# Where the last norm's token rows are fetched, and which rows of the last expert are finished first, in a diffusion step with a mixture of experts

## The chip, the cores and the metric

The kernel runs on one core of a Trainium2 chip. The metric is the device time of one launch in microseconds (us). The kernel before took 1339.0 us (the median of three runs, 1337.55 to 1339.12).

A few words that the text uses: TensorE is PE in the profile (PEld is its weight load), VectorE is DVE, ScalarE is ACT, GpSimd is POOL, and SyncE is SP, which computes nothing here and only issues transfers. PSUM is where TensorE leaves its sums.

## The reference

One inference step: a trunk layer over 512 sample tokens and 128 prompt tokens of width 1024, then a routed layer of 16 experts, then a last norm. What bears on the change is the end:

```python
def ec_moe(x, router_w, w1, w3, w2):
    probs = softmax(xf @ router_w)
    gates, idx = lax.top_k(probs.T, cap)        # cap: 64 sample tokens, 16 prompt tokens per expert
    xe = xf[idx]
    h = silu(xe @ w1) * (xe @ w3)               # 1024 -> 2048, for each of 16 experts
    ye = (h @ w2) * gates                       # 2048 -> 1024
    return zeros.at[idx].add(ye)

x = x + gate2 * ec_moe(h2, ...)
y = x * rsqrt(mean(x * x) + EPS) * final_norm_w   # rmsnorm of every token row
```

The outputs are the normed rows of the prompt and of the sample tokens, and two final states of the trunk's scan.

## The kernel before

**The trunk** takes about the first quarter of the time and is not touched. It leaves the token rows (5 tiles of 128 rows by 1024; tile 4 holds the prompt rows) in DRAM, in `acc_dram`.

**The experts.** Each expert has 12 weight pieces of 2 MB: eight for w1 and w3 (`m` 0 to 7), four for w2 (`m` 8 to 11). SP issues them in order into a ring of six slots (L596) and waits, before each, until TensorE has read the piece six before it. Expert 0 stands by itself, experts 1 to 14 are a loop, and the last one (15, `LAST`) stands by itself. Every expert but the last adds its rows to `acc_dram` with a scatter from GpSimd (L749).

**The last expert.** Its rows are not scattered into `acc_dram`. GpSimd gathers the rows concerned (`last_rows`, the sample rows, L753; `last_rows_p`, the 16 prompt rows, L756) as soon as expert 14's scatter has landed, VectorE adds the last expert's products to them, and they get their own norm. TensorE takes the products in this order: the sample part of w2's first piece (`down_sample(0)`, L1289), the prompt part of all four pieces (`down_prompt(i)`, L1300), and then the sample part of the other three. So the prompt products (`Y_B` in PSUM) are complete first and the sample products (`Y_A`) last.

**The tiles.** Meanwhile all 640 rows as experts 0 to 14 left them are normed too: SP fetches the five tiles of `acc_dram` into `x` (L641, `acc_loaded`), ScalarE squares and sums each (L1638, `y_squared`), VectorE makes mean and reciprocal (L1664, L1665, `y_recip`), ScalarE takes the root (L1640, `y_rs`), VectorE scales the five tiles (`scale_tiles`, L2165, `y_ready`), and SP stores them (L650, `y_saved`). The rows that the last expert has also changed are stale in these stores and are overwritten: GpSimd scatters the prompt rows (L764) and the sample rows (L768) over them. L764 waits for `y_saved` of all five tiles and for `last_p_scaled`; L768 stands behind L764 in GpSimd's program and waits for `last_scaled`.

**VectorE at the end.** `finish_prompt_rows` adds the rows (L2171), waits for ScalarE's square (L1643), makes mean and reciprocal, waits for the root (L1645) and scales (L2175). `finish_sample_rows` reads `Y_A` (L2181), adds (L2185), waits for ScalarE's square (L1647) and a small TensorE product that sums two half rows (L1369), makes mean and reciprocal, waits for the root (L1649) and scales (L2190).

**What sets the order** is the order in which the code is written. Every engine works through its own program in order, and whatever waits for a semaphore holds up all that stands behind it on its engine. No planner takes part.

Of the kernel before, what the change touches and what calls it, by code (L numbers as in the profile page):

```python
# [18 lines left out]
ACT = mybir.ActivationFunctionType  # L19
# [5 lines left out]
P = 128  # L25
# [3 lines left out]
TILES = (SAMPLE + PROMPT) // P  # L29
# [11 lines left out]
CAP_S, CAP_P = 2 * SAMPLE // EXPERTS, 2 * PROMPT // EXPERTS  # L41
# [3 lines left out]
LAST = EXPERTS - 1  # L45
# [116 lines left out]
OUT_ORDER = [ST] + list(range(ST))  # L162
# [33 lines left out]
def trunk_kernel(nc, x_prompt, x_sample, s0_f, s0_b, c, c_ctx, ada_w, ada_b, norm1_w, w_in, wa2_f, ba_f,  # L196
                 wa2_b, ba_b, gla_norm_w, sgu_norm_w, sgu_ws, sgu_bs, w_out, norm2_w, router_w, w1, w3, w2,
                 final_norm_w, table, pos_row, pos_col, y_prompt, y_sample, new_f, new_b):
    with ExitStack() as ctx:
# [27 lines left out]
        x = sb("x", TILES * D)[:].rearrange("p (t d) -> p t d", t=TILES)  # L227
# [338 lines left out]
        def _(sp):  # L566
# [68 lines left out]
                    wait_expert_chunk_read(sp, m - RING, expert)  # L635
                    load_expert_chunk(m, expert)
            for m in range(EXPERT_LOADS):
                if m == 9:
                    sp.wait_ge(acc_saved, 16 * (TILES + LAST))
                    for t in OUT_ORDER:  # L640
                        sp.dma_start(x[:, t, :], acc_dram[t * P:(t + 1) * P, :]).then_inc(acc_loaded[t], 16)  # L641
                wait_expert_chunk_read(sp, m - RING, LAST)
                load_expert_chunk(m, LAST)


            for i, t in enumerate(OUT_ORDER):
                sp.wait_ge(y_ready, i + 1)
# [725 lines left out]
        def _(act):  # L1373
# [259 lines left out]
                expert_work(expert)  # L1633
            expert_work(LAST)

            for i, t in enumerate(OUT_ORDER):
                act.wait_ge(acc_loaded[t], 16)
                nc.scalar.activation(y_out[:, t, :], x[:, t, :], ACT.Square, accum_out=stats[:, 130 + i:131 + i]).then_inc(y_squared, 1)  # L1638
            act.wait_ge(y_recip, 1)
            nc.scalar.activation(stats[:, 140:140 + TILES], stats[:, 135:135 + TILES], ACT.Sqrt).then_inc(y_rs, 1)  # L1640

            act.wait_ge(last_p_added, 1)
            nc.scalar.activation(last_sq_p, last_rows_p, ACT.Square, accum_out=stats[0:CAP_P, 145:146]).then_inc(last_p_squared, 1)  # L1643
            act.wait_ge(last_p_recip, 1)
            nc.scalar.activation(stats[0:CAP_P, 148:149], stats[0:CAP_P, 147:148], ACT.Sqrt).then_inc(last_p_rs, 1)  # L1645
            act.wait_ge(last_added, 1)
            nc.scalar.activation(last_sq, last_rows, ACT.Square, accum_out=stats[:, 125:126]).then_inc(last_squared, 1)  # L1647
            act.wait_ge(last_recip, 1)
# [4 lines left out]
        def _(dve):  # L1653
# [8 lines left out]
            def mean_recip(out, sums, width, then, own=link):  # L1662

                own(nc.vector.tensor_scalar(out, sums, 1.0 / width, EPS, ALU.mult, ALU.add))  # L1664
                nc.vector.reciprocal(out, out).then_inc(then, 1)  # L1665
# [492 lines left out]
            def scale_tiles():  # L2158

                dve.wait_ge(y_squared, TILES)  # L2160
                mean_recip(stats[:, 135:135 + TILES], stats[:, 130:130 + TILES], D, y_recip, link_final)
                dve.wait_ge(final_loaded, 16)
                dve.wait_ge(y_rs, 1)
                for i, t in enumerate(OUT_ORDER):
                    nc.vector.scalar_tensor_tensor(y_out[:, t, :], x[:, t, :], stats[:, 140 + i:141 + i], final_w, ALU.mult, ALU.mult)\  # L2165
                        .then_inc(y_ready, 1)

            def finish_prompt_rows():

                dve.wait_ge(last_p_loaded, 16)  # L2170
                nc.vector.tensor_tensor(last_rows_p, last_rows_p, last_y_p[0:CAP_P], ALU.add).then_inc(last_p_added, 1)  # L2171
                dve.wait_ge(last_p_squared, 1)
                mean_recip(stats[0:CAP_P, 147:148], stats[0:CAP_P, 145:146], D, last_p_recip, link_final)
                dve.wait_ge(last_p_rs, 1)
                nc.vector.scalar_tensor_tensor(last_rows_p, last_rows_p, stats[0:CAP_P, 148:149], final_w[0:CAP_P], ALU.mult, ALU.mult)\  # L2175
                    .then_inc(last_p_scaled, 1)
# [15 lines left out]
            def expert_work(expert, last=False):  # L2192
# [9 lines left out]
                for part in range(PARTS):  # L2202
# [5 lines left out]
                    wait_role_stored(dve, f"R3_{part}", expert)  # L2208
                    nc.vector.transpose(h[:, :, part * PART:(part + 1) * PART], h_rows[:, part, :].rearrange("p (c a) -> p c a", a=PART))\  # L2209
                        .then_inc(h_turned[part], 1)  # L2210
                if last:
                    scale_tiles()
                else:
                    dve.wait_ge(gathered, 16 + 48 + expert * 48)
                    for part in range(PARTS):
                        ins = nc.vector.transpose(xe[:, :, part * PART:(part + 1) * PART], xq[:, part, :].rearrange("p (i k) -> p k i", k=KT))  # L2216
                    ins.then_inc(xq_turned, 1)
                    dve.wait_ge(xq_turned, expert + 1)
                    kinds = ((slice(0, CAP_S), 0), (slice(CAP_S, PADDED), 1))
                    for slots, w in kinds:  # L2220
                        shape = [P, KT, slots.stop - slots.start]
                        ins = nc.vector.tensor_tensor(xe[:, :, slots], xe[:, :, slots], amp2[:, :, w:w + 1].to_broadcast(shape), ALU.mult)
                    link_expert(ins)
                    for slots, w in kinds:
                        shape = [P, KT, slots.stop - slots.start]
                        ins = nc.vector.tensor_tensor(xe[:, :, slots], xe[:, :, slots], mod[:, SHIFT2:SHIFT2 + KT, w:w + 1].to_broadcast(shape),
                                                      ALU.add)
                    ins.then_inc(xe_ready, 1)
# [13 lines left out]
                if last:  # L2242
                    link_final(ins)
                    finish_prompt_rows()
                    finish_sample_rows()
                    return
                wait_role_filled(dve, "Y_A", expert)
# [38 lines left out]
```

## Time and profile before

| | |
|---|---|
| median of three runs | 1339.0 us |
| the profiled execution: its own time, its span | 1340.9 us, 1339.1 us |
| TensorE busy | 1323.7 us (99% of the span) |
| VectorE busy | 462.6 us (35%) |
| ScalarE busy | 170.5 us (13%) |
| GpSimd busy | 109.4 us (8%) |
| moved by the DMA engines | 470.88 MB, 352 GB/s over the span |
| the last weight piece, from issue to landing | 1297.22 to 1319.1 us |
| last matmul of the last expert | ends at 1331.35 us |

The span runs from the first to the last instruction of the profiled execution; the own time of that execution also holds what lies around it. A time such as 1319.1 us is counted from the span's start. The mean busy shares are averages over the trunk, sixteen experts and the end; the change lies in the last 60 us alone.

### The profile page before, as it was taken

How to read it: one execution, taken by the hardware profiler on the slowest of the kernel's cores; microseconds unless marked ns; L12 is line 12 of the kernel's file. 1: busy time of each engine (PE TensorE's matmuls, PEld its weight loads, DVE VectorE, ACT ScalarE, POOL GpSimd, SP SyncE). 2: the span in 40 equal slices, each digit the busy share in tenths (PEclk: the TensorE clock that was granted, in tenths of full speed). 3: DMA queues.
4: the chain of work that ended last, by engine and by line, in shares of the span. 5: the costliest groups of instructions: out<-in, count | busy, mean ns of one | idle time of the engine just before them, and what ended most of it. 6: DMA issues, size and time to landing. Idle time of an engine off the chain costs nothing.

```text
span 1339.1 us, 24267 instructions
## 1 busy us (share of the span) xinstructions
PE 1323.7 (99%) x10761; PEld 470.6 (35%) x10761; DVE 462.6 (35%) x850; ACT 170.5 (13%) x277; POOL 109.4 (8%) x119
## 2 busy tenths in 40 slices
PE   9999999999999999999999999999999999999996
PEld 3544555554333333333333333333333333333331
DVE  3189886977130403122121304031221212130405
ACT  3443624123100000000000000000000000000002
POOL 0300000110100101010000001010100000000000
PEclk9999999999999999999999999999999999999999
DMA  9733731247799999999999999999999999999995
GB/s 316 252 126 134 251 111 36 83 157 288 278 424 421 424 419 415 431 417 428 418 427 419 426 419 426 420 421 426 414 431 415 429 418 426 420 427 418 430 406 221
DMA packets 64349, 470.88 MB, mean 352 GB/s; under 512 B 5685, under 2 KB 17794, under 8 KB 39738
## 3 DMA queue, kind: packets, MB, share of 16 engines
q1 hardware_dynamic: 57184, 451.56, 81.4%
q0 software_dynamic: 6320, 18.45, 4.6%
q8 instruction: 26, 0.43, 0.1%
q10 hardware_dynamic: 810, 0.37, 0.1%
q14 instruction: 9, 0.07, 0.0%
HBM read 456.99 MB, written 13.37 MB: 351 GB/s over the span
## 4 chain that ended last, share of the span: by engine, by line
PE 95%; DMA 2%; DVE 1%; issue 1%; ACT 0%; POOL 0%; POOLq 0%; DVEq 0%
PE psum L1273 49%; PE psum L1289 15%; PE psum L1300 8%; PE psum L843 8%; PE psum L1117 4%; PE psum L885 2%; PE psum L1059 2%; DMA ring<-in_exp_w_dram 2%; PE psum L850 1%; PE psum L930 1%; PE psum L1069 1%; PE psum L863 1%; PE psum L786 0%; PE psum L1023 0%; PE psum L1028 0%
## 5 line engine op out<-in xcount | busy, mean ns | idle before, releaser
L1273 PE MATMUL psum<-ring,both 128*32 128x512 f32 x6144 | 664.8, 593 | 0.6 <-issue 0.6
L1273 PEld LDWEIGHTS psum<-ring,both 128*32 128x32 f32 x6144 | 199.4, 110 | 457.5 <-issue 457.3
L2205 DVE TENSOR_TENSOR both<-both,psum 128x512 f32<-128x512 f32 x48 | 50.4, 1051 | 555.7 <-PE psum L1273 555.7
L1289 PE MATMUL psum<-ring,both 128*32 128x512 f32 x2048 | 231.1, 592 | 0.0
L1626 ACT ACTIVATE both<-psum 128x512 f32<-128x512 f32 x48 | 28.7, 597 | 934.0 <-PE psum L1273 934.0
L1300 PE MATMUL psum<-ring,both 128*32 128x512 f32 x1024 | 118.6, 592 | 2.9 <-DMA ring<-in_exp_w_dram 2.9
L1289 PEld LDWEIGHTS psum<-ring,both 128*32 128x32 f32 x2048 | 66.6, 110 | 153.2 <-issue 153.2
L843 PE MATMUL psum<-ring,feat 128*128 128x512 f32 x240 | 104.3, 593 | 0.0
L701 POOL DMA_INDIRECT both<-xn_dram,both x45 | 49.5, 1101 | 579.2 <-DVE both L2216 569.8
L2235 DVE SCALAR_TENSOR_TENSOR both<-psum,both 64x512 f32<-64x512 f32 x32 | 24.0, 749 | 177.7 <-PE psum L1300 177.5
L1117 PE MATMUL psum<-ring,both 128*128 128x512 f32 x160 | 71.2, 596 | 0.0
L843 PEld LDWEIGHTS psum<-ring,feat 128*128 128x128 f32 x240 | 45.1, 190 | 55.2 <-issue 55.1
L1300 PEld LDWEIGHTS psum<-ring,both 128*32 128x32 f32 x1024 | 33.1, 110 | 80.1 <-issue 75.4
L1712 DVE SCALAR_TENSOR_TENSOR both<-ring,silu_c,both 128x512 f32<-128x512 f32 x88 | 58.8, 744 | 0.0
L749 POOL DMA_INDIRECT acc_dram<-both x15 | 22.0, 1467 | 267.2 <-DVE both L2250 267.2
L1117 PEld LDWEIGHTS psum<-ring,both 128*128 128x128 f32 x160 | 29.5, 190 | 32.9 <-issue 32.9
L2209 DVE STREAM_TRANSPOSE both<-both 128x512 f32<-128x512 f32 x48 | 34.2, 712 | 1.7
L885 PE MATMUL psum<-feat,ring 128*128 128x512 f32 x64 | 29.1, 597 | 0.0
L1059 PE MATMUL psum<-feat,ring 128*128 128x512 f32 x64 | 28.0, 596 | 0.0
L2216 DVE STREAM_TRANSPOSE both<-both 128x256 f32<-128x256 f32 x45 | 25.2, 605 | 0.0
L2250 DVE SCALAR_TENSOR_TENSOR both<-psum,both 64x512 f32<-64x512 f32 x30 | 22.5, 750 | 6.7 <-PE psum L1289 6.5
L2241 DVE TENSOR_TENSOR both<-both 32x512 f32<-32x512 f32 x32 | 21.9, 684 | 0.8
(312 smaller groups left out, 632.3 us busy)
## 6 DMA issues: line engine op xcount, KB each, us to landing
ring<-in_exp_w_dram SPq DMA_DIRECT2D x192, 2048.0 KB, 17.6
ring<-in_ada_w_dram SPq DMA_DIRECT2D x8, 2048.0 KB, 7.9
ring<-in_w_in_dram SPq DMA_DIRECT2D x4, 2048.0 KB, 14.5
ring<-in_ada_w_dram SPq DMA_DIRECT2D x6, 1024.0 KB, 11.3
ring<-in_w_out_dram SPq DMA_DIRECT2D x2, 2048.0 KB, 12.2
acc_dram<-x POOLq DMA_DIRECT2D x5, 512.0 KB, 3.1
xn_dram<-feat POOLq DMA_DIRECT2D x5, 512.0 KB, 5.2
x<-acc_dram SPq DMA_DIRECT2D x5, 512.0 KB, 18.0
```

The lines of the kernel that those rows point to most:

```text
L701: pool.indirect_dma_start(out=xq[:, part, :], out_offset=None, in_=xn2_dram.rearrange("t (a n) -> (t a) n", a=4), in_offset=bass.IndirectO ...
L843: mm = nc.tensor.matmul(bank(n), hT[:, kt, t * P:(t + 1) * P], w[:, kt, :], start=(kt == 0), stop=(kt == KT - 1))
L885: return nc.tensor.matmul(bank(JOB["qkS", m]), w[:, kt, m * P:(m + 1) * P], hT[:, kt, 0:SAMPLE], start=(kt == 0), stop=(kt == KT - 1))
L1059: mm = nc.tensor.matmul(bank(n), w[:, kt, gr * P:(gr + 1) * P], hT[:, kt, 0:SAMPLE], start=(kt == 0), stop=(kt == KT - 1))
L1117: mm = nc.tensor.matmul(bank(n), mix, w[:, kt, :], start=(kt == 0), stop=(kt == KT - 1))
L1273: mm = nc.tensor.matmul(role_bank(role)[f4 * PART:(f4 + 1) * PART, :], xe[:, kt, part * PART:(part + 1) * PART], w[:, kt % 2, f4 * 512:(f4 ...
L1289: mm = nc.tensor.matmul(role_bank("Y_A")[at:at + PART, :], h[:, c, part * PART:(part + 1) * PART], w[:, f, half * 512:(half + 1) * 512], s ...
L1300: mm = nc.tensor.matmul(role_bank("Y_B")[at:at + PART, :], h[:, c, 2 * PART:PADDED], w[:, f + odd, half * 512:(half + 1) * 512], start=(c ...
L1626: role_stored(nc.scalar.activation(silu_h[:, r % 2, :], role_bank(role), ACT.Silu), role)
L1712: ins = nc.vector.scalar_tensor_tensor(sums[:, w, :], rows[:, kt, :], scale, sums[:, w, :], ALU.mult, ALU.add)
L2205: role_stored(nc.vector.tensor_tensor(h_rows[:, part, :].rearrange("p (c a) -> p a c", a=PART), silu_h[:, part % 2, :].rearrange("p (a c) ...
L2209: nc.vector.transpose(h[:, :, part * PART:(part + 1) * PART], h_rows[:, part, :].rearrange("p (c a) -> p c a", a=PART))\
```

## The change

Three things are moved. SP fetches the five tiles behind the last expert's last weight piece, no longer ahead of its tenth. ScalarE's square and root for the prompt rows stand ahead of the squares of the tiles. On VectorE, `scale_tiles` is called behind `finish_prompt_rows` and ahead of `finish_sample_rows`, and the wait for the norm's weight row (`final_loaded`) goes along to the first scaling. No instruction is added or removed.

```diff
@@ SP, the last expert's weight pieces
             for m in range(EXPERT_LOADS):
-                if m == 9:
-                    sp.wait_ge(acc_saved, 16 * (TILES + LAST))
-                    for t in OUT_ORDER:
-                        sp.dma_start(x[:, t, :], acc_dram[t * P:(t + 1) * P, :]).then_inc(acc_loaded[t], 16)
                 wait_expert_chunk_read(sp, m - RING, LAST)
                 load_expert_chunk(m, LAST)
-
+            sp.wait_ge(acc_saved, 16 * (TILES + LAST))
+            for t in OUT_ORDER:
+                sp.dma_start(x[:, t, :], acc_dram[t * P:(t + 1) * P, :]).then_inc(acc_loaded[t], 16)
@@ ScalarE, behind the last expert's work
+            act.wait_ge(last_p_added, 1)
+            nc.scalar.activation(last_sq_p, last_rows_p, ACT.Square, accum_out=stats[0:CAP_P, 145:146]).then_inc(last_p_squared, 1)
+            act.wait_ge(last_p_recip, 1)
+            nc.scalar.activation(stats[0:CAP_P, 148:149], stats[0:CAP_P, 147:148], ACT.Sqrt).then_inc(last_p_rs, 1)
             for i, t in enumerate(OUT_ORDER):
                 act.wait_ge(acc_loaded[t], 16)
                 nc.scalar.activation(y_out[:, t, :], x[:, t, :], ACT.Square, ...).then_inc(y_squared, 1)
             act.wait_ge(y_recip, 1)
             nc.scalar.activation(stats[:, 140:140 + TILES], stats[:, 135:135 + TILES], ACT.Sqrt).then_inc(y_rs, 1)
-            act.wait_ge(last_p_added, 1)
-            nc.scalar.activation(last_sq_p, last_rows_p, ACT.Square, ...).then_inc(last_p_squared, 1)
-            act.wait_ge(last_p_recip, 1)
-            nc.scalar.activation(stats[0:CAP_P, 148:149], stats[0:CAP_P, 147:148], ACT.Sqrt).then_inc(last_p_rs, 1)
@@ VectorE, expert_work(LAST, last=True)
-                if last:
-                    scale_tiles()
-                else:
+                if not last:
...
                 if last:
                     link_final(ins)
                     finish_prompt_rows()
+                    scale_tiles()
                     finish_sample_rows()
                     return
```

ScalarE's program behind the last `silu` of the last expert, before. `acc_loaded4` is the prompt tile, `last_p_added` says that VectorE has added the prompt rows:

```order
L1638 ACTIVATE feat,stats<-x 128x1024 [waits acc_loaded4]
L1638 ACTIVATE feat,stats<-x 128x1024 [waits acc_loaded0]
L1638 ACTIVATE feat,stats<-x 128x1024 [waits acc_loaded1]
L1638 ACTIVATE feat,stats<-x 128x1024 [waits acc_loaded2]
L1638 ACTIVATE feat,stats<-x 128x1024 [waits acc_loaded3]
L1640 ACT_TABLE_LOAD
L1640 ACTIVATE stats<-stats 128x5 [waits y_recip]
L1643 ACTIVATE both,stats<-both 16x1024 [waits last_p_added]
L1645 ACTIVATE stats<-stats 16x1 [waits last_p_recip]
L1647 ACTIVATE both,stats<-both 128x512 [waits last_added]
```

The same place on ScalarE in the changed kernel (its lines are numbered anew: 1635 is the prompt rows' square, 1640 the tiles'):

```order
L1635 ACTIVATE both,stats<-both 16x1024 [waits last_p_added]
L1637 ACT_TABLE_LOAD
L1637 ACTIVATE stats<-stats 16x1 [waits last_p_recip]
L1640 ACTIVATE feat,stats<-x 128x1024 [waits acc_loaded4]
L1640 ACTIVATE feat,stats<-x 128x1024 [waits acc_loaded0]
L1640 ACTIVATE feat,stats<-x 128x1024 [waits acc_loaded1]
L1640 ACTIVATE feat,stats<-x 128x1024 [waits acc_loaded2]
L1640 ACTIVATE feat,stats<-x 128x1024 [waits acc_loaded3]
L1642 ACTIVATE stats<-stats 128x5 [waits y_recip]
L1645 ACTIVATE both,stats<-both 128x512 [waits last_added]
```

The prompt rows' two instructions have moved to the front, the load of the root's table has gone with the first root, and the five squares of the tiles now stand behind a wait for `last_p_added`.

VectorE's program behind the last transpose of the last expert, before. `psum_filled7` says that the prompt products `Y_B` are complete, `psum_filled6` the sample products `Y_A`:

```order
L1664 TENSOR_SCALAR stats<-stats 128x5 [waits y_squared]
L1665 RECIPROCAL stats<-stats 128x5 [waits vec_final_step]
L2165 SCALAR_TENSOR_TENSOR feat<-x,stats,both 128x1024 [waits y_rs,final_loaded]
L2165 SCALAR_TENSOR_TENSOR feat<-x,stats,both 128x1024 x4
L2235 SCALAR_TENSOR_TENSOR both<-psum,both 64x512 [waits psum_filled7,acc_saved]
L2235 SCALAR_TENSOR_TENSOR both<-psum,both 64x512
L2241 TENSOR_TENSOR both<-both 32x512 [waits psum_stored7]
L2241 TENSOR_TENSOR both<-both 32x512
L2171 TENSOR_TENSOR both<-both 16x1024 [waits last_p_loaded,vec_final_step]
L1664 TENSOR_SCALAR stats<-stats 16x1 [waits last_p_squared]
L1665 RECIPROCAL stats<-stats 16x1 [waits vec_final_step]
L2175 SCALAR_TENSOR_TENSOR both<-both,stats 16x1024 [waits last_p_rs]
```

The same place in the changed kernel, from the prompt rows' addition to the reading of `Y_A` (2168 was 2171, 2162 was 2165, 2179 was 2181):

```order
L2168 TENSOR_TENSOR both<-both 16x1024 [waits last_p_loaded,vec_final_step]
L1662 TENSOR_SCALAR stats<-stats 16x1 [waits last_p_squared]
L1663 RECIPROCAL stats<-stats 16x1 [waits vec_final_step]
L2173 SCALAR_TENSOR_TENSOR both<-both,stats 16x1024 [waits last_p_rs,final_loaded]
L1662 TENSOR_SCALAR stats<-stats 128x5 [waits y_squared]
L1663 RECIPROCAL stats<-stats 128x5 [waits vec_final_step]
L2162 SCALAR_TENSOR_TENSOR feat<-x,stats,both 128x1024 [waits y_rs]
L2162 SCALAR_TENSOR_TENSOR feat<-x,stats,both 128x1024 x4
L2179 SCALAR_TENSOR_TENSOR both<-psum,both 128x512 [waits psum_filled6]
```

The tiles' mean, reciprocal and five scalings have moved from ahead of the prompt products to between the prompt rows and the sample rows.

## Rows read from the trace of the kernel before

**Rows 1.** The page: busy time, share of the span and instructions of each engine.

```profile
PE 1323.7 (99%) x10761; PEld 470.6 (35%) x10761; DVE 462.6 (35%) x850; ACT 170.5 (13%) x277; POOL 109.4 (8%) x119
```

**Rows 2.** The chain that ended last, in order of time: start us, us, what.

```profile
1297.22 21.87 DMA ring<-in_exp_w_dram
```

**Rows 3.** Timeline of SP's issues: start us, us, engine, line, operation, tiles, count.

```profile
1286.92 10.63 SPq L596 DMA_DIRECT2D ring<-in_exp_w_dram  x3
1314.53 5.58 SPq L650 DMA_DIRECT2D out_dram<-feat  x5
```

**Rows 4.** Line 641, the last tile's fetch alone: duration ns, start; time to landing.

```profile
L641 SPq DMA_DIRECT2D x<-acc_dram x1: 432/432/432, 1284.8 to 1284.8; - x1
...
DMA to landing us min/median/max: 19.6/19.6/19.6
```

**Rows 5.** Line 596, the piece issued at 1286.92 alone: its time to landing.

```profile
DMA to landing us min/median/max: 22.4/22.4/22.4
```

**Rows 6.** Timeline of PEld around the last two pieces' prompt products; brackets: idle before.

```profile
1313.28 0.13 PEld L1300 LDWEIGHTS psum<-ring,both 128*32 128x32 f32 x4 [0.30 <-issue]
...
1319.13 0.16 PEld L1300 LDWEIGHTS psum<-ring,both 128*32 128x32 f32 x8 [3.85 <-DMA ring<-in_exp_w_dram]
...
1320.44 0.13 PEld L1289 LDWEIGHTS psum<-ring,both 128*32 128x32 f32 x4 [0.30 <-issue]
```

**Rows 7.** Timeline of ACT and DVE in the tiles' norm.

```profile
1306.30 1.05 ACT L1638 ACTIVATE feat<-x 128x1024 f32<-128x1024 f32 x1
...
1311.61 1.28 ACT L1640 ACT_TABLE_LOAD   x1
...
1312.91 0.21 ACT L1640 ACTIVATE stats<-stats 128x5 f32<-128x5 f32 x1
1313.22 6.07 DVE L2165 SCALAR_TENSOR_TENSOR feat<-x,stats,both 128x1024 f32<-128x1024 f32 x5 [1.20 <-ACT stats L1640]
```

**Rows 8.** Timeline of ACT and DVE over the prompt rows.

```profile
1321.19 1.51 DVE L2235 SCALAR_TENSOR_TENSOR both<-psum,both 64x512 f32<-64x512 f32 x2 [1.91 <-PE psum L1300]
...
1324.15 1.21 DVE L2171 TENSOR_TENSOR both<-both 16x1024 f32<-16x1024 f32 x1
...
1325.39 1.06 ACT L1643 ACTIVATE both<-both 16x1024 f32<-16x1024 f32 x1 [12.28 <-DVE both L2171]
...
1326.36 0.18 ACT L1643 ACTIVATION_READ_ACCUMULATOR both<-both 16x1 f32 x1
...
1326.93 0.20 ACT L1645 ACTIVATE stats<-stats 16x1 f32<-16x1 f32 x1 [0.39 <-DVE stats L1665]
...
1327.17 1.27 DVE L2175 SCALAR_TENSOR_TENSOR both<-both,stats 16x1024 f32<-16x1024 f32 x1 [0.27 <-ACT stats L1645]
```

**Rows 9.** Timeline over the sample rows and the last scatter.

```profile
1331.42 0.75 DVE L2181 SCALAR_TENSOR_TENSOR both<-psum,both 128x512 f32<-128x512 f32 x1 [2.98 <-PE psum L1289]
...
1333.80 0.35 PE L1369 MATMUL psum<-stats,fold 128*128 128x1 f32 x2 [2.44 <-ACT both L1647]
...
1334.82 0.75 DVE L2190 SCALAR_TENSOR_TENSOR both<-both,stats 128x512 f32<-128x512 f32 x1 [0.27 <-ACT stats L1649]
1335.85 1.02 POOL L768 DMA_INDIRECT out_dram<-both  x1 [5.70 <-DVE both L2190]
```

**Rows 10.** Line 650, all five stores of the tiles: their time to landing.

```profile
DMA to landing us min/median/max: 3.8/4.2/5.9
```

**Rows 11.** Line 695, five stores of 512 KB in the trunk: their time to landing.

```profile
DMA to landing us min/median/max: 3.0/3.1/11.3
```

**Rows 12.** Timeline of POOL: both gathers of the last rows, and the prompt rows' scatter.

```profile
1278.44 1.01 POOL L753 DMA_INDIRECT both<-acc_dram,both  x1 [8.89 <-DMA acc_dram<-both]
1279.75 0.90 POOL L756 DMA_INDIRECT both<-acc_dram,both  x1 [0.30 <-issue]
1329.28 0.86 POOL L764 DMA_INDIRECT out_dram<-both  x1 [48.63 <-DVE both L2175]
```

**Rows 13.** One stretch: busy us and count of each engine, granted clock, DMA share, GB/s.

```profile
1334.00:1336.00 2.00, 0.15 (x2) 0.07 (x1) 1.08 (x3) 0.20 (x1) 0.15 (x1) 0.58 0.00 0
```

More of the change, by code:

```diff
@@ L1640, in _ @@
             nc.scalar.activation(stats[:, 140:140 + TILES], stats[:, 135:135 + TILES], ACT.Sqrt).then_inc(y_rs, 1)
-            act.wait_ge(last_p_added, 1)
-            nc.scalar.activation(last_sq_p, last_rows_p, ACT.Square, accum_out=stats[0:CAP_P, 145:146]).then_inc(last_p_squared, 1)
-            act.wait_ge(last_p_recip, 1)
-            nc.scalar.activation(stats[0:CAP_P, 148:149], stats[0:CAP_P, 147:148], ACT.Sqrt).then_inc(last_p_rs, 1)
             act.wait_ge(last_added, 1)
@@ L2161, in scale_tiles @@
                 mean_recip(stats[:, 135:135 + TILES], stats[:, 130:130 + TILES], D, y_recip, link_final)
-                dve.wait_ge(final_loaded, 16)
                 dve.wait_ge(y_rs, 1)
@@ L2173, in finish_prompt_rows @@
                 mean_recip(stats[0:CAP_P, 147:148], stats[0:CAP_P, 145:146], D, last_p_recip, link_final)
+                dve.wait_ge(final_loaded, 16)
                 dve.wait_ge(last_p_rs, 1)
```

## The prediction

> **What bounds the kernel now.** I read the page first: TensorE is busy for 99% of the span [rows 1], so only its waits and what runs behind its last product can be won or lost. Then the chain of waits, and in it the last 60 us, since the change touches nothing earlier. The reader should see one wait that isn't TensorE's own work: the last weight piece, issued at 1297.22, lands 21.87 us later, at 1319.09 [rows 2]. The timeline of the weight loads shows what it costs. A group of four loads comes every 0.43 us (0.13 and 0.30 idle). From the group at 1313.28 to the first one of the sample products at 1320.44 are 7.16 us [rows 6]. Eight groups lie between (the prompt products of the last two pieces, 16 each, four to a group), so unhindered it is nine pitches, 3.87 us. The stall is 7.16 - 3.87 = 3.29 us.
>
> Behind the stall comes a serial end: the prompt products are read at 1321.19 [rows 8], the sample products at 1331.42, the last scatter starts at 1335.85 [rows 9], and the span ends 3.25 us later, at 1339.1. The tiles' own norm, from 1306.30 to 1319.29 [rows 7], is hidden now: ScalarE and VectorE have nothing else to do while TensorE works and waits. That cover is what the change gives up.
>
> **Part 1, SP: the tiles behind the last piece.** Line 641's five issues go past three weight pieces. The last tile, issued at 1284.8, lands 19.6 us later, at 1304.4 [rows 4]. The piece behind it, issued at 1286.92 [rows 3], lands after 22.4 us, at 1309.3 [rows 5]. So 2048 KB took 4.9 us behind a tile, and the five tiles of 512 KB are worth 2560/2048 x 4.9 = 6.1 us. Each of the last three pieces lands that much earlier, the last one at 1313.0. TensorE wants it at 1313.28 + 5 x 0.43 = 1315.4, so there are 2.4 us to spare and the stall goes whole: -3.29 us for both sets of products. It can't be more, since TensorE wants the piece no earlier. SP now waits for `acc_saved` behind the last piece; that was met before 1278.44, when the gathers started [rows 12], and costs nothing. Behind it are only the stores. The tiles land from about 1314.2 to 1319.1 (1313.0 + 6.1).
>
> At the queue a rule bears on this. The trace shows pieces and tiles landing in the order of issue. The Trainium skill, "DMA: Bandwidth & Descriptors", section "Queues, rings and completion order", says the same of the start of descriptors on one engine, but also that completions of one issuing engine are not first in, first out. By its first half the last piece is clear of the tiles; by its second it need not be, which is the first rival below.
>
> **Part 2, ScalarE: prompt rows first.** Two costs. First, all five squares now stand behind `last_p_added` and the prompt root. With the stall gone, VectorE reads the prompt products at 1321.19 - 3.29 = 1317.90. By [rows 8] the prompt square starts 4.20 us later (1325.39 - 1321.19) and ends at +5.35 (1326.36 + 0.18), so at 1323.25. Second, the table load, 1.28 us [rows 7], now lies here: it doesn't wait for the semaphore of the root (in the tiles' norm it starts at 1311.61, when the squares end). So it runs 1323.27 to 1324.55, beside VectorE's two small instructions, and the root ends at 1324.77. Without the load it would have ended at 1317.90 + 5.94 = 1323.84, so this costs 0.93 us. The tiles have long landed (5.7 us to spare), and the five squares take 1311.61 - 1306.30 = 5.31 us: to 1330.08.
>
> A rule speaks for more. Between load and root the row leaves 0.02 us (1311.61 + 1.28 to 1312.91) [rows 7]. The Trainium skill, "ScalarE: Activation LUTs", section "What ACT_TABLE_LOAD costs", puts a drain of about 1380 ns beside the load of about 1283 ns. By the row the sum stays; by the rule the tiles' norm would be later by about 1.4 us. I take the row.
>
> **Part 3, VectorE: tiles between prompt and sample rows.** From the end of a square over mean, reciprocal and root to the scaling are 1327.17 - 1326.54 = 0.63 us without a load [rows 8], so the five scalings start at 1330.71 and with their 6.07 us [rows 7] end at 1336.78. Queued behind them is the reading of `Y_A` (complete at about 1328.1) and the whole sample part, for which ScalarE, TensorE's last small product and the last scatter wait. It starts at 1336.8, not at 1331.42 - 3.29 = 1328.13. `L2190` ends 4.15 us after that start (1334.82 + 0.75 - 1331.42), and the scatter could start 4.43 us after it (1335.85 - 1331.42) [rows 9]: 1341.2. That alone makes an end at 1344.5. Moving `final_loaded` costs nothing: that row was fetched in the first third of the kernel.
>
> **Part 4, the stores and the order of the scatters.** The five stores are not added, but lose their cover. The last is issued at 1336.8. Its landing took 3.8 to 5.9 us beside the weights [rows 10]; the same 512 KB took 3.0 to 3.1 us in the trunk where nothing was in the way, up to 11.3 otherwise [rows 11]. Nothing else is under way now and a store is shorter (about 1.2 us by part 1) than a scaling, so I take 3.1: 1339.9; the ends are 3.0 and 5.9. GpSimd's scatter L764 waits for it and started 0.84 us after its releaser before (L2175 ended at 1328.44), L768 0.28 us after its own; I take 0.6. L768 stands behind L764, and two such issues follow at 1279.75 - 1278.44 = 1.31 us [rows 12]. So L768 starts at 1339.9 + 0.6 + 1.31 = 1341.8, 0.6 later than VectorE would let it, and the span ends 3.25 us later: 1345.1. That the prompt rows are finished ahead (1326.1 for 1328.44) brings nothing, because L764 waits for the stores.
>
> TensorE idles 11 us ahead of its small product. Before, after 2.44 us idle, it took 0.35 us [rows 9], and the mean granted clock of the stretch around the end was 0.58 [rows 13]. At the lower level (1.2 of 2.4 GHz) it and its weight load of 0.30 us cost at most 0.65 us more, and at least nothing. I take nothing, since up to 0.6 us hides behind the stores.
>
> **The sum.** Span 1339.1 to 1345.1: -3.29 for the stall, +8.67 for the sample part behind the tiles (1336.8 - 1328.13), +0.6 for the stores. The profiled execution's own time is 1340.9 and would be 1346.9. It lies 1.9 above the median of 1339.0; the same +6.0 gives **1345.0 us**. The ends: stores at 3.0 and 0.28 of lag give 1344.5 for the median, 5.9 and 0.84 give 1348.0.
>
> **Rival 1: the stall stays.** The tiles share the engines with the last piece, which is issued just ahead of them, and it lands at 1319.1 as before. For it speaks that the stores issued from 1314.53 [rows 3] landed from 3.8 us on [rows 10], the first at 1318.3, ahead of the last piece. Against it, that a piece behind the tiles took 4.9 us, its full share of the stream. Everything is then 3.29 later: 1348.3.
>
> **Rival 2: a longer load of the table.** In its new place it is followed by a pause as long as itself, 1.28 us. Only the 0.02 us after it speaks against. 1346.3.
>
> **Rival 3, the other side: the last products carry the end, and the stall's 3.29 comes out whole,** 1335.7. It needs the passes over the tiles to be much shorter once the DMA engines are quiet. The point from which it isn't slower: the sample part starts by 1331.42, so squares and scalings must lose 5.4 of their 11.4 us. Against it: the prompt rows' square (1.06) and scaling (1.27) ran when the weights had ended [rows 8] and are as long as those of a tile (1.05, and 6.07 for five) [rows 7].
>
> **How the numbers follow.** Forecast 0.83, rival 1 0.09, rival 2 0.04, rival 3 and its half-way cases 0.04. A measurement here tells 0.2%, 2.7 us, from no change. The forecast and the first two rivals are all slower by more; of the last 0.04 I give 0.01 to faster and 0.03 to no change. The range runs from 1342.9, below the lowest sum (1344.5) by the scatter of the runs (1.6 us), to 1348.5, which takes in rival 1 and the late stores.
>
> **What would show it.** Right: no wait of TensorE for a weight piece in the last expert; the prompt products read near 1317.9; the table load between the prompt square and its root; squares of the tiles from about 1324.8, their scalings from 1330.7 to 1336.8; L2179 (the former L2181) released by nothing but its place; L764 near 1340.5, released by the stores, and L768 right behind it. Wrong: a wait for the last piece that stays (rival 1), a gap behind the table load (rival 2), tile passes under 1 us each (rival 3), or a last scatter that starts before 1339.

## The result and the profile after

The changed kernel takes 1345.07 us (median of six runs, 1344.79 to 1348.03) against 1339.09 us (six runs, 1337.55 to 1341.57). The ratio is 1.0047, with a 95% interval from 1.0037 to 1.0057: slower by 5.0 to 7.6 us. The forecast was 1345.0 us.

The profiled execution has a span of 1343.1 us. That is only 4.0 us more than 1339.1, because this execution was 1.5 us ahead already when the last expert's second half began. So the traces are compared from one point that no variant touches: the start of the last expert's first sample product (`down_sample(0)`). In the trace of before it is here (timeline of PE: start us, us, what):

```profile
1307.27 3.62 PE L1289 MATMUL psum<-ring,both 128*32 128x512 f32 x32
```

From there to the end of the span are 31.83 us. In the changed kernel the same stretch begins and goes on like this (timeline of PE and SP; L1287 is the former L1289, L1298 the former L1300, L642 the former L641):

```profile
1296.07 2.33 SPq L642 DMA_DIRECT2D x<-acc_dram  x5
...
1305.76 3.62 PE L1287 MATMUL psum<-ring,both 128*32 128x512 f32 x32
...
1309.19 7.05 PE L1298 MATMUL psum<-ring,both 128*32 128x512 f32 x64
...
1316.06 10.48 PE L1287 MATMUL psum<-ring,both 128*32 128x512 f32 x96
```

From 1305.76 to 1343.1 are 37.34 us: +5.51 (spans are recorded to 0.1 us; up to the start of the last scatter the difference is 5.52, from 28.58 to 34.10). All 64 matmul rows of the prompt products are now one piece without a gap, where before 48 of them were followed by the wait that [rows 6] show. The last piece's time from issue to landing, 21.87 us in [rows 2], is now

```profile
L596 SPq DMA_DIRECT2D ring<-in_exp_w_dram x1: 328/328/328, 1295.7 to 1295.7; - x1
...
DMA to landing us min/median/max: 15.7/15.7/15.7
```

and that is 6.2 us less. What the stall gave back, the end took, and more. This is the chain that ended last, from the prompt square on, in order of time (start us, us, what):

```profile
1320.58 1.15 ACT both L1635 x2
1321.72 0.02 issue
1321.74 1.28 ACT L1637
1323.02 0.01 issue
1323.04 0.20 ACT stats L1637
1323.24 5.20 ACT feat L1640 x10
...
1330.34 4.88 DVE feat L2162 x4
1335.21 0.02 issue
1335.23 3.04 DMA out_dram<-feat
1338.26 0.27 issue
1338.53 0.86 POOL out_dram L762
```

The reader should see that TensorE's sample products are nowhere in it, though the last of them ended only at 1326.54 (1316.06 + 10.48): prompt square, table load, root, the five squares of the tiles (x10 with their accumulator reads), the five scalings. Before, the squares [rows 7] were not in this chain. From 1335.23 on the view goes over the last store and the prompt rows' scatter. What released the last scatter was VectorE's last scaling (L2188, in the last row below), and that stands behind the sample part and TensorE's small product; the run with TensorE busy shows below that this second way was the longer one, by little. The rows that answer to [rows 8], [rows 9] and [rows 12], from the timeline (L2231 reads the prompt products, L2162 scales the tiles, L2179 starts the sample part, L1367 is the small product):

```profile
1316.38 1.51 DVE L2231 SCALAR_TENSOR_TENSOR both<-psum,both 64x512 f32<-64x512 f32 x2 [8.51 <-PE psum L1298]
...
1329.13 6.07 DVE L2162 SCALAR_TENSOR_TENSOR feat<-x,stats,both 128x1024 f32<-128x1024 f32 x5 [0.28 <-ACT stats L1642]
...
1335.23 0.75 DVE L2179 SCALAR_TENSOR_TENSOR both<-psum,both 128x512 f32<-128x512 f32 x1
...
1337.61 0.56 PE L1367 MATMUL psum<-stats,fold 128*128 128x1 f32 x2 [11.07 <-ACT both L1645]
...
1338.83 0.75 DVE L2188 SCALAR_TENSOR_TENSOR both<-both,stats 128x512 f32<-128x512 f32 x1 [0.27 <-ACT stats L1647]
1339.86 1.02 POOL L766 DMA_INDIRECT out_dram<-both  x1 [0.47 <-DVE both L2188]
```

The sample part (L2179) has no idle time before it: it waited only for its place behind the scalings.

### The profile page after: what moved, and what is told of

It reads as the page before. It is cut to its first block, busy times and chain, and to the rows that moved or that the text cites. A ratio compares the mean times of both kernels' runs of the same rounds, so it can differ in the third digit from the quotient of the medians.

```text
span 1343.1 us, 24267 instructions
## 1 busy us (share of the span) xinstructions
PE 1319.6 (98%) x10761; PEld 470.0 (35%) x10761; DVE 462.3 (34%) x850; ACT 170.4 (13%) x277; POOL 109.3 (8%) x119
## 4 chain that ended last, share of the span: by engine, by line
PE 95%; DVE 2%; DMA 1%; SPq 1%; ACT 1%; issue 1%; POOLq 0%; POOL 0%; DVEq 0%
PE psum L1271 49%; PE psum L1287 16%; PE psum L1298 8%; PE psum L841 8%; PE psum L1115 4%; PE psum L883 2%; PE psum L1057 2%; DMA ring<-in_ada_w_dram 1%; PE psum L1067 1%; PE psum L928 1%; SPq L578 1%; PE psum L784 0%; PE psum L1021 0%; ACT feat L1640 0%; PE psum L1026 0%
## 5 line engine op out<-in xcount | busy, mean ns | idle before, releaser
L1287 PE MATMUL psum<-ring,both 128*32 128x512 f32 x2048 | 231.1, 592 | 0.0
L1287 PEld LDWEIGHTS psum<-ring,both 128*32 128x32 f32 x2048 | 66.6, 110 | 153.2 <-issue 153.2
L1298 PE MATMUL psum<-ring,both 128*32 128x512 f32 x1024 | 118.3, 592 | 0.0
L2231 DVE SCALAR_TENSOR_TENSOR both<-psum,both 64x512 f32<-64x512 f32 x32 | 24.0, 750 | 184.3 <-PE psum L1298 184.0
L1298 PEld LDWEIGHTS psum<-ring,both 128*32 128x32 f32 x1024 | 33.3, 110 | 76.6 <-issue 76.6
```

The costliest lines, as they stand in the source:

```text
L1287: mm = nc.tensor.matmul(role_bank("Y_A")[at:at + PART, :], h[:, c, part * PART:(part + 1) * PART], w[:, f, half * 512:(half + 1) * 512], s ...
L1298: mm = nc.tensor.matmul(role_bank("Y_B")[at:at + PART, :], h[:, c, 2 * PART:PADDED], w[:, f + odd, half * 512:(half + 1) * 512], start=(c ...
```

## The experiments

Two theories stood. The one of the forecast: the tiles' fetch costs a stall of 3.3 us where it was, its new place gives that back, and VectorE's and ScalarE's passes over the tiles, put between the prompt rows and the sample rows, cost 8.7 us. The rival: the late fetch itself, with its late stores, is what costs.

The variants were timed in five rounds beside the kernel before on the same chip (1339.67 us in the first set of four, 1338.72 us in the second, of the last three timed ones), all but the two with a busy TensorE, which ran once each. The ratio is against the kernel before of the same set. "Stretch" is the time in the trace from the start of the last expert's first sample product to the end of the span, which is known to 0.1 us.

| kernel | time us | ratio and 95% interval | stretch us | against before |
|---|---|---|---|---|
| before | 1339.09 | | 31.83 | |
| changed | 1345.07 | 1.0047, 1.0037 to 1.0057 | 37.34 | +5.51 |
| only the fetch moved | 1343.24 | 1.0028, 1.0018 to 1.0037 | 35.67 | +3.84 |
| only the orders moved | 1349.20 | 1.0073, 1.0060 to 1.0085 | 40.13 | +8.30 |
| changed, squares first | 1341.19 | 1.0009, 1.0000 to 1.0019 | 33.44 | +1.61 |
| before, no fetch (output incomplete) | 1334.90 | 0.9967, 0.9955 to 0.9979 | 28.54 | -3.29 |
| two tiles ahead | 1335.43 | 0.9976, 0.9965 to 0.9987 | 28.56 | -3.27 |
| prompt scaling in the gap | 1338.38 | 0.9987, 0.9977 to 0.9997 | 29.32 | -2.51 |
| three tiles ahead | 1336.15 | 0.9981, 0.9969 to 0.9992 | 29.14 | -2.69 |
| changed, TensorE busy (12 matmuls) | 1346.46, one run | | 37.14 | +5.31 |

**Only the fetch moved.** SP as changed, the rest as before.

```diff
-                if m == 9:
-                    sp.wait_ge(acc_saved, 16 * (TILES + LAST))
-                    for t in OUT_ORDER:
-                        sp.dma_start(x[:, t, :], acc_dram[...]).then_inc(acc_loaded[t], 16)
                 wait_expert_chunk_read(sp, m - RING, LAST)
                 load_expert_chunk(m, LAST)
+            sp.wait_ge(acc_saved, 16 * (TILES + LAST))
+            for t in OUT_ORDER:
+                sp.dma_start(x[:, t, :], acc_dram[...]).then_inc(acc_loaded[t], 16)
```

> Only SP's part of the change: the five tiles fetched behind the last weight piece, ScalarE and VectorE ordered as in the kernel before. Theory (the stall of 3.3 us goes, and what counts is how long VectorE is away from the last products): the last tile lands about where the last piece landed before, its square ends 1.3 us later, then root with table load, five scalings of 6.07 us, and only then the prompt products. Counted in the frame of the trace of before: scalings 1322.0 to 1328.1, sample part from about 1335.3 for 1331.42: slower by about 4 us, 1343.1 us. Rival (the late fetch with its late stores is what costs in the changed kernel): this one has the same late fetch, so it is as slow as the changed kernel, 1345 us.

Measured: 1343.24 us, 3.84 us more in the stretch. The timeline shows why (its L1636 is the tiles' square, L2163 their scaling, L2233 the first reading of the prompt products):

```profile
1312.50 1.06 ACT L1636 ACTIVATE feat<-x 128x1024 f32<-128x1024 f32 x1 [7.54 <-DMA x<-acc_dram]
...
1317.53 1.06 ACT L1636 ACTIVATE feat<-x 128x1024 f32<-128x1024 f32 x1
...
1320.30 6.07 DVE L2163 SCALAR_TENSOR_TENSOR feat<-x,stats,both 128x1024 f32<-128x1024 f32 x5 [1.20 <-ACT stats L1638]
...
1326.29 1.50 DVE L2233 SCALAR_TENSOR_TENSOR both<-psum,both 64x512 f32<-64x512 f32 x2
```

The squares now follow the landings, 1.26 us apart, and VectorE is away until 1326.29, though TensorE had the prompt products complete near 1316.4. With the orders of before, the late fetch turns -3.3 into +3.8. The rival said 1345, as slow as the changed kernel, and is off by 2 us; in the stretch the changed kernel takes 1.67 us more, which the late fetch by itself doesn't explain.

**Only the orders moved.** ScalarE and VectorE as changed, SP as before (against the changed kernel).

```diff
+                if m == 9:
+                    sp.wait_ge(acc_saved, 16 * (TILES + LAST))
+                    for t in OUT_ORDER:
+                        sp.dma_start(x[:, t, :], acc_dram[...]).then_inc(acc_loaded[t], 16)
                 wait_expert_chunk_read(sp, m - RING, LAST)
                 load_expert_chunk(m, LAST)
-            sp.wait_ge(acc_saved, 16 * (TILES + LAST))
-            for t in OUT_ORDER:
-                sp.dma_start(x[:, t, :], acc_dram[...]).then_inc(acc_loaded[t], 16)
```

> Only the orders on ScalarE and VectorE of the change, the tiles fetched ahead of the tenth weight piece as in the kernel before. Theory: the stall of 3.3 us is back and the passes over the tiles still stand behind the prompt rows, so everything behind the stall is 3.3 us later than in the changed kernel: 1348.3 us. Rival (late fetch): the tiles are there early and the time falls back to about that of before, 1339 to 1341 us.

Measured: 1349.20 us, +8.30 in the stretch, the slowest of all, with tiles that were there long before they were used. That the late fetch is what costs in the changed kernel is out: with the same orders, the early fetch is slower. The +8.30 is 0.5 short of 5.51 + 3.29, because in this execution TensorE idled less:

```profile
1318.50 1.92 PE L1300 MATMUL psum<-ring,both 128*32 128x512 f32 x16 [2.57 <-DMA ring<-in_exp_w_dram]
```

In the trace of before the same wait was 2.94 us, and the 48 rows ahead of it took 5.49 us for 5.33 here, with a wait for the piece before the last: 0.37 + 0.16 us. How far the stream of weights is behind TensorE differs by some tenths between executions; what sets that was not settled.

**Changed, squares first.** The five squares ahead of the prompt rows' square, the tiles' root where the change puts it (against the changed kernel).

```diff
+            for i, t in enumerate(OUT_ORDER):
+                act.wait_ge(acc_loaded[t], 16)
+                nc.scalar.activation(y_out[:, t, :], x[:, t, :], ACT.Square, ...).then_inc(y_squared, 1)
             act.wait_ge(last_p_added, 1)
             nc.scalar.activation(last_sq_p, last_rows_p, ACT.Square, ...).then_inc(last_p_squared, 1)
             act.wait_ge(last_p_recip, 1)
             nc.scalar.activation(stats[0:CAP_P, 148:149], ..., ACT.Sqrt).then_inc(last_p_rs, 1)
-            for i, t in enumerate(OUT_ORDER):
-                ...
             act.wait_ge(y_recip, 1)
```

> The changed kernel with ScalarE's five squares of the tiles ahead of the prompt rows' square again; the tiles' root stays behind the prompt rows' root. Fetch and VectorE as changed. Theory: the squares (5.3 us) leave the path, but VectorE has the prompt rows' scaling (1.3 us) in front of the tiles now: the scalings start 8.9 us behind the reading of the prompt products instead of 12.8, so 3.9 us faster than the changed kernel, 1341.2 us. Rival (the fetch or the stores bind): no change, 1345 us.

Measured: 1341.19 us; the stretch is 3.90 us shorter than the changed kernel's. So the place of the squares on ScalarE is worth 3.9 us of the change, and the fetch, which is as late here, costs none of it: the last square ended before the prompt rows were added.

```profile
1316.77 1.06 ACT L1636 ACTIVATE feat<-x 128x1024 f32<-128x1024 f32 x1
...
1320.08 1.05 ACT L1638 ACTIVATE both<-both 16x1024 f32<-16x1024 f32 x1 [2.16 <-DVE both L2168]
1321.25 1.28 ACT L1640 ACT_TABLE_LOAD   x1
...
1324.70 6.07 DVE L2162 SCALAR_TENSOR_TENSOR feat<-x,stats,both 128x1024 f32<-128x1024 f32 x5 [0.28 <-ACT stats L1642]
```

**Before, no fetch.** SP doesn't fetch and ScalarE doesn't wait for it; the tiles' rows then lack what the experts added.

```diff
-                if m == 9:
-                    sp.wait_ge(acc_saved, 16 * (TILES + LAST))
-                    for t in OUT_ORDER:
-                        sp.dma_start(x[:, t, :], acc_dram[...]).then_inc(acc_loaded[t], 16)
...
-                act.wait_ge(acc_loaded[t], 16)
                 nc.scalar.activation(y_out[:, t, :], x[:, t, :], ACT.Square, ...)
```

> The kernel before without the fetch of the tiles: the norm of the tiles works on the rows that the trunk left in x, so the output lacks the experts' part for the rows that the last expert did not take. It gives the price of the stall by itself. Theory: TensorE's wait for the last piece (3.3 us) is gone and nothing else changes, 1335.8 us. Rival: the prompt rows, the stores or the scatters take its place, and less than 1.5 us comes out, 1337.6 us or more.

Measured: 1334.90 us, -3.29 in the stretch, the size of the stall read from [rows 6] (up to the last scatter's start it is -3.30). No other wait took its place on the way to the end, though one appeared (L2230 reads the prompt products, L2176 starts the sample part):

```profile
1319.10 1.50 DVE L2230 SCALAR_TENSOR_TENSOR both<-psum,both 64x512 f32<-64x512 f32 x2
...
1328.02 0.75 DVE L2176 SCALAR_TENSOR_TENSOR both<-psum,both 128x512 f32<-128x512 f32 x1 [1.67 <-PE psum L1285]
```

VectorE, still scaling tiles, read the prompt products at 1319.10, 1.3 us later than it could have: in the changed kernel it reads them 10.62 us after the first sample product, here 11.94 (1319.10 - 1307.16). The 1.67 us that it then waits for the sample products show that this cost nothing.

**Two tiles ahead** (against the kernel before, shortened; the lines that begin with @@ and the comment only tell what follows). Since the last piece had 2.4 us to spare and a tile takes 1.2 us of the stream, two tiles should fit ahead of it. VectorE's work on the other three is 3.7 us instead of 6.1.

```diff
+AHEAD = 2
+TILE_GROUPS = ((0, AHEAD), (AHEAD, TILES))
...
                 if m == 9:
                     sp.wait_ge(acc_saved, 16 * (TILES + LAST))
-                    for t in OUT_ORDER:
+                    for t in OUT_ORDER[:AHEAD]:
                         sp.dma_start(x[:, t, :], acc_dram[...]).then_inc(acc_loaded[t], 16)
                 wait_expert_chunk_read(sp, m - RING, LAST)
                 load_expert_chunk(m, LAST)
+            for t in OUT_ORDER[AHEAD:]:
+                sp.dma_start(x[:, t, :], acc_dram[...]).then_inc(acc_loaded[t], 16)
@@ ScalarE: squares and root for each group, then the prompt rows
@@ VectorE
                 if last:
-                    scale_tiles()
+                    tile_recips(0)
+                    scale_tiles(0)
...
                     link_final(ins)
+                    tile_recips(1)
                     finish_prompt_rows()     # adds, then scale_tiles(1), then the prompt rows' own norm
```

> Two tiles fetched ahead of the tenth weight piece, three behind the last; the first two are squared, rooted and scaled while TensorE still works towards the prompt products, the other three get their mean and reciprocal ahead of the prompt rows' addition and are scaled between it and the prompt rows' scaling. Theory (2.4 us of slack at the last piece, 1.2 us for each tile ahead of it, and VectorE free for 1328.1 in the frame of the trace of before): two tiles just fit, no stall, and the sample part starts as soon as the last products are there: 3.3 us faster than before, the ratio 0.9975. Rival (VectorE's work between the prompt products and the last products doesn't fit, or the last piece is late after all): 1 to 2 us faster at most, ratio 0.9985 to 1.

Measured: 1335.43 us against 1338.72 us, ratio 0.9976 (0.9965 to 0.9987): faster than before and than the changed kernel, and all of the stall comes out (-3.27 in the stretch). Among the kernels with the full output it has the lowest median, but timing doesn't tell it from three tiles ahead. The timeline shows how tight it is (L1303 is the former L1300, L2193 the sample part's start):

```profile
1313.29 0.13 PEld L1303 LDWEIGHTS psum<-ring,both 128*32 128x32 f32 x4 [0.30 <-DMA ring<-in_exp_w_dram]
...
1315.76 1.51 DVE L2248 SCALAR_TENSOR_TENSOR both<-psum,both 64x512 f32<-64x512 f32 x2 [5.32 <-PE psum L1303]
...
1320.12 3.66 DVE L2176 SCALAR_TENSOR_TENSOR feat<-x,stats,both 128x1024 f32<-128x1024 f32 x3
...
1324.30 1.27 DVE L2187 SCALAR_TENSOR_TENSOR both<-both,stats 16x1024 f32<-16x1024 f32 x1 [0.27 <-ACT stats L1650]
1325.99 0.75 DVE L2193 SCALAR_TENSOR_TENSOR both<-psum,both 128x512 f32<-128x512 f32 x1 [0.42 <-PE psum L1292]
```

The last piece lands just as its weight load is due (no idle beyond the usual 0.30), and VectorE waits 0.42 us for the last products.

**The prompt rows' scaling in the gap.** On top of the former, the prompt rows' scaling moved out of `finish_prompt_rows` to behind the sample rows' addition (one of the changed places, against the former).

```diff
                 nc.vector.tensor_tensor(last_rows, last_rows, last_out, ALU.add).then_inc(last_added, 1)
+                scale_prompt_rows()
                 dve.wait_ge(last_total, 1)
```

> The former with the prompt rows' scaling (1.27 us) moved from ahead of the sample part into the 1.3 us in which VectorE waits for the square and TensorE's small product. Theory: if VectorE was late for the last products, what it was late by (up to 1.3 us) comes out; if it was in time, nothing changes, since the scatter of the prompt rows still ends about when the sample rows are ready. I expect within 0.5 us of the former. Rival: the prompt rows' scatter, now later, holds up the last one, and it is 0.5 to 1 us slower.

Measured: the rival. The ratios, 0.9976 and 0.9987, have intervals that overlap; it is the stretch that shows it, 0.76 us longer. VectorE had been in time, so there was nothing to win, and the prompt rows' scatter came late:

```profile
1331.63 0.75 DVE L2206 SCALAR_TENSOR_TENSOR both<-both,stats 128x512 f32<-128x512 f32 x1 [0.27 <-ACT stats L1654]
1331.74 1.38 POOL L767 DMA_INDIRECT out_dram<-both  x1 [50.93 <-DVE both L2190]
1333.42 1.02 POOL L771 DMA_INDIRECT out_dram<-both  x1 [0.30 <-issue]
```

The sample rows were ready at 1332.38 (1331.63 + 0.75), the last scatter began at 1333.42, 0.30 us behind the one in front of it, where 0.28 us after the sample rows would have been 1332.66. Two things made the scatter in front end so late. It started 0.84 us after its release, where I had 0.3, and it ran 1.38 us (1.30 with two tiles ahead, 0.86 in the trace of before). Why it ran longer is open.

**Three tiles ahead.** `AHEAD = 3`.

> Three tiles ahead of the tenth piece, two behind the last. Theory: the third tile takes the last piece 1.2 us past the point at which TensorE wants it, a stall of 1.2 to 1.3 us, so 2.0 us faster than before, ratio 0.9985, and 1.2 us slower than with two ahead. Rival (the slack is larger than 2.4 us, or VectorE is what binds with two): the same as with two ahead or faster.

Measured: ratio 0.9981 (0.9969 to 0.9992), which the timing doesn't tell from two tiles; in the stretch 0.58 us slower than two, half of what I expected. The direction is right, TensorE does wait for the last piece:

```profile
1317.09 0.13 PEld L1303 LDWEIGHTS psum<-ring,both 128*32 128x32 f32 x4 [0.30 <-issue]
1318.35 0.16 PEld L1303 LDWEIGHTS psum<-ring,both 128*32 128x32 f32 x8 [1.13 <-DMA ring<-in_exp_w_dram]
...
1319.66 0.13 PEld L1292 LDWEIGHTS psum<-ring,both 128*32 128x32 f32 x4 [0.30 <-issue]
```

The load is 0.83 us late (1.13 less the usual 0.30), but then eight weight loads go at once, and four groups take 1.31 us (1318.35 to 1319.66) instead of 1.72: TensorE catches up 0.41 us and loses 0.42. The same catch-up is in [rows 6] (1319.13 to 1320.44), and there the pitch count had it in already. The other 0.2 us: TensorE's small product took 0.56 us here, 0.35 with two tiles.

**Changed, TensorE busy** (against the changed kernel). To see whether the granted clock and the stores bear on the end: extra matmuls behind TensorE's last product, into a bank that nobody reads. A first try had 96 of them.

```diff
             expert_products(LAST, last=True)
+            wait_role_stored(pe, "R1_1", LAST)
+            for i in range(12):          # 96 in the first try
+                nc.tensor.matmul(role_bank("R1_1")[0:PART, :], h[:, 0, 0:PART], chunk(...)[:, 0:512], start=(i == 0), stop=(i == 11))
             pe.wait_ge(fold_ready, 1)
```

> The changed kernel with 96 more matmuls of 32 columns by 512 behind TensorE's last product, into a bank that nobody reads, so that TensorE doesn't idle for 11 us ahead of its small product (10.3 us of work). Theory (the small product is slow because the granted clock has fallen to the lower level, and the last scatter is held by two things that come due together, the sample rows and the scatter in front of it): the small product takes 0.35 us for 0.56, the sample rows are ready 0.2 us earlier, and the last scatter starts no earlier than before, 1.3 us behind the start of the one in front. Rival (the stores don't hold it): the last scatter follows the sample rows by 0.28 us and all the 0.2 us come out.

The first try missed its aim: the 96 took 82.6 us, not 10.3, 0.86 us for each (two rows of 0.43). The kernel's own rows come four in 0.43 us, each of the four into another quarter of the output, while all 96 went into the same quarter; that this is the reason was not tried by itself. The small product came far too late (span 1413.6 us). With 12 of them:

> The changed kernel with 12 more matmuls behind TensorE's last product instead of the 96 of the run before, in which one took 0.86 us (82.6 us for 96), so that they end (10.3 us) about when the small product is wanted. Theory: the small product takes 0.35 us for 0.56, the sample rows are ready 0.2 us earlier, but the last scatter still starts 1.3 us behind the start of the prompt rows' scatter, which waits for the stores: nothing is gained. Rival (the stores don't hold it): the last scatter follows the sample rows by 0.28 us, 0.2 us come out.

Measured, in one execution (timeline; L1366 are the added matmuls, two rows each):

```profile
1328.06 10.46 PE L1366 MATMUL psum<-ring,both 128*32 128x512 f32 x24
...
1336.94 0.75 DVE L2182 SCALAR_TENSOR_TENSOR both<-psum,both 128x512 f32<-128x512 f32 x1
...
1339.31 0.35 PE L1370 MATMUL psum<-stats,fold 128*128 128x1 f32 x2 [0.79 <-ACT both L1648]
...
1340.23 0.86 POOL L762 DMA_INDIRECT out_dram<-both  x1 [59.38 <-DMA out_dram<-feat]
1340.33 0.75 DVE L2191 SCALAR_TENSOR_TENSOR both<-both,stats 128x512 f32<-128x512 f32 x1 [0.27 <-ACT stats L1650]
1341.40 1.02 POOL L766 DMA_INDIRECT out_dram<-both  x1 [0.30 <-DVE both L2191]
```

The small product is back at 0.35 us, as expected, with a granted clock of 1.00 from 1338.00 to 1340.00. But the stretch is 0.20 us shorter (37.14 for 37.34): the rival of this run was right, all but a rest. Both kernels reach the sample part equally long after the point of comparison (29.48 and 29.47 us), so the difference lies behind it. From there to the last scatter are 4.46 us here and 4.63 in the changed kernel: 0.17 of the 0.21 us by which the small product is shorter. The other 0.04 us went to the scatter in front, which ended at 1341.09, while the sample rows were ready at 1341.08; the last scatter started 0.32 us after them, not 0.28. Two scatters thus follow at 1.17 us (1340.23 to 1341.40), not at the 1.31 of the gathers [rows 12]. In the changed kernel the sample rows are ready 0.2 us later, so there the stores held nothing up, though by little.

## Why the prediction was right

The sum in the prediction was -3.29, +8.67 and +0.6, in all +6.0. The trace shows +5.51, within the interval of the timed runs (5.0 to 7.6), so that the forecast of 1345.0 stands 0.1 us from the median is partly luck: the sum is 0.5 us too high in the trace, and two of its terms are off in opposite directions. Point by point, in the stretch:

- **The stall.** -3.29 predicted. The prompt products are read 10.62 us after the first sample product (1316.38 - 1305.76); before it was 13.92 (1321.19 - 1307.27): -3.30. The kernel without the fetch gives the same from the other side. Rival 1, the tiles beside the last piece, is out: the piece landed 6.2 us earlier, 6.1 predicted.
- **ScalarE.** From reading the prompt products to the tiles' first scaling 12.75 us (1329.13 - 1316.38); 12.81 predicted (1330.71 - 1317.90). The table load sits behind the prompt square and the root follows it by 0.02 us (1323.02 to 1323.04). Rival 2, a pause behind the load, is out, and with it the drain that the Trainium skill ("ScalarE: Activation LUTs", "What ACT_TABLE_LOAD costs") names: no run here shows it.
- **VectorE.** The five scalings took 6.07 us, as beside the weights; rival 3 is out. The sample part began 18.85 us after the reading of the prompt products (1335.23 - 1316.38), 18.9 predicted. Before, that distance was 10.23 us (1331.42 - 1321.19), so the tiles' passes put 8.62 us on the path.
- **The stores: mis-sized.** Predicted +0.6, measured nothing. The last store's landing was right (3.04 us for 3.1), but GpSimd started 0.27 us after it, not 0.6, and the run with TensorE busy has two scatters at 1.17 us, not 1.31. The last scatter started 0.28 us after the sample rows (1339.86, ready at 1339.58), as before.
- **The small product: mis-sized the other way.** I took nothing, because the stores would hide it. The granted clock was 0.50 around it (the lower of the two levels, 1.2 GHz), it took 0.56 us for 0.35, and with nothing to hide it, it cost 0.20 us (4.63 us from the sample part's start to the last scatter, for 4.43). The 0.58 of [rows 13] doesn't tell of the small product of before: that stretch begins at 1334.00, the product at 1333.80, and the row around its start has 1.00 (the first one here, of the trace of before). The other three are stretches of the changed kernel behind TensorE's last sample product. A row has the busy us and count of PE, PEld, DVE, ACT and POOL, the granted clock, the DMA share and GB/s:

```profile
1333.00:1334.00 1.00, 0.20 (x2) 0.23 (x2) 0.00 (x0) 0.66 (x2) 0.00 (x0) 1.00 0.00 0
```

```profile
1327.00:1331.00 4.00, 0.00 (x0) 0.00 (x0) 2.23 (x4) 1.64 (x5) 0.00 (x0) 0.79 0.00 0
1331.00:1336.00 5.00, 0.00 (x0) 0.00 (x0) 4.95 (x5) 0.00 (x0) 0.00 (x0) 0.50 0.96 384
1336.00:1339.00 3.00, 0.56 (x2) 0.50 (x2) 1.18 (x4) 0.93 (x3) 0.47 (x1) 0.50 0.59 234
```

So -3.30 + 8.62 + 0.20 = +5.52, against 5.51 measured.

Neither half of the change is good by itself as it stands. The fetch alone costs 3.8 us, since VectorE still does the tiles first and now gets them late; the two orders alone cost 8.3 us; together they cost 5.5. ScalarE's order and VectorE's were not each run alone. The stall was worth removing, but by moving three tiles of five, with VectorE's and ScalarE's work split the same way.

## What to carry to other kernels

A transfer moved behind another gives back at most the wait that it caused (3.3 of 6.2 us here), and as many bytes can stay ahead as the next transfer has to spare; count the pitches of the waiting engine to get both. Before work is moved from beside a busy engine to behind it, add up what stands between that engine's last two results: on an in-order engine all of it delays the last one, and a pass on a second engine (the squares, 3.9 us) counts as soon as it stands behind the same wait.

## What the runs showed of the hardware that was not expected

- GpSimd's prompt-row scatter started 0.84 us after its releaser when that was VectorE's scaling (before, only the fetch moved, no fetch, and the scaling in the gap) and 0.26 to 0.27 us after it when that was the landing of the last store (changed, squares first, only the orders moved, two and three tiles ahead, TensorE busy). Why is open.
- After a late weight piece TensorE regained 0.40 to 0.41 us over the next four groups of loads, in three traces (before, only the orders moved, three tiles ahead).
- TensorE's small product took 0.56 us with three tiles ahead and 0.35 us with two, both after 2.44 us idle. The granted clock of the stretch was 0.50 in the one and 1.00 in the other; with the same idle time before it, the clock had fallen already in the one and not yet in the other:

```profile
1333.00:1334.00 1.00, 0.56 (x2) 0.49 (x2) 0.32 (x2) 0.00 (x0) 0.00 (x0) 0.50 0.00 0
```

```profile
1328.00:1329.00 1.00, 0.35 (x2) 0.30 (x2) 0.21 (x2) 0.22 (x2) 0.20 (x1) 1.00 0.30 45
```

(The first row is of the kernel with three tiles ahead, the second of the one with two.)
- In the profiled executions of the timed kernels the last expert's first sample product began between 1305.1 and 1309.4 us. That difference arises ahead of the point of comparison, and the timed runs of one kernel spread by 3 to 6.5 us; so differences of some tenths are read here from the stretch and not from the times. Why the executions differ ahead of that point was not settled.
